# A hybrid encoder layer with 16 experts: expert weights loaded two chunks at a time

## What is computed

```
gates, idx = top_k(transpose(softmax(x @ w_router)), 64)      # each of 16 experts takes its 64 best tokens
xe  = x[idx]                                                  # 64 x 1024
hid = silu(xe @ w_gate[e]) * (xe @ w_up[e])                   # 1024 x 2048 each
ye  = (hid @ w_down[e]) * gates                               # 2048 x 1024
y[idx] += ye
```

## Time and profile before

| | us |
|---|---|
| median of 3 runs | 1295.26 |
| lowest, highest | 1293.75, 1296.32 |
| the profiled execution: its own time | 1294.17 |
| its span (first to last instruction) | 1292.4 |
| TensorE busy with matmuls | 1152.6 (89%) |
| packets of the SP queue's loads, share of 16 DMA engines | 81.0% |
| HBM read | 439.65 MB |

### The profile page before, as it was taken

One profiled execution on the slowest core, in us unless ns is written; L12 is line 12 of the kernel. 1 busy time (PEld: TensorE's weight loads), 2 busy tenths in 40 slices (PEclk: granted clock), 3 DMA queues, 4 the chain that ended last, 5 costly groups with the idle time before them and its releaser, 6 DMA issues.

```text
span 1292.4 us, 13555 instructions
## 1 busy us (share of the span) xinstructions
PE 1152.6 (89%) x5620; PEld 576.8 (45%) x5620; DVE 264.4 (20%) x465; ACT 191.4 (15%) x352; POOL 124.5 (10%) x61
## 2 busy tenths in 40 slices
PE   8999998989499999999889978997998899789874
PEld 6876777888453343333224322422432243234221
DVE  2012377637610020020002002000200020020005
ACT  4223434142100000000000001000000100010003
POOL 4412225321003000000000000000000000000003
PEclk9999999999699999999999999999999999999997
DMA  9432222163769999999999999999999999999992
GB/s 370 160 117 88 99 75 112 69 254 166 293 235 427 426 424 428 429 428 426 429 429 430 426 428 429 430 427 427 429 429 427 427 429 430 427 427 428 430 425 97
DMA packets 38030, 442.19 MB, mean 342 GB/s; under 512 B 6512, under 2 KB 6640, under 8 KB 10736
## 3 DMA queue, kind: packets, MB, share of 16 engines
q1 hardware_dynamic: 34512, 438.55, 81.0%
q10 hardware_dynamic: 3488, 3.22, 0.8%
HBM read 439.65 MB, written 2.10 MB: 342 GB/s over the span
## 4 chain that ended last, share of the span: by engine, by line
PE 72%; DMA 17%; DVE 6%; ACT 3%; issue 1%; POOL 1%; SPq 0%; POOLq 0%; ACTq 0%; DVEq 0%
PE bank L970 25%; DMA ring<-in_w_exp 16%; PE bank L992 16%; PE bank L929 5%; PE bank L1002 4%; PE bank L667 2%; PE bank L669 2%; PE bank L672 2%; PE bank L656 2%; ACT yt L618 1%; PE bank L979 1%; PE bank L804 1%; PE bank L805 1%; PE bank L806 1%; PE bank L648 1%
## 5 line engine op out<-in xcount | busy, mean ns | idle before, releaser
L970 PE MATMUL bank<-ring,yt 128*64 128x512 f32 x2048 | 452.7, 595 | 43.8 <-DMA ring<-in_w_exp 43.8
L970 PEld LDWEIGHTS bank<-ring,yt 128*64 128x64 f32 x2048 | 142.9, 137 | 336.0 <-issue 256.4
L992 PE MATMUL bank<-ring,yt 128*64 128x512 f32 x992 | 221.0, 595 | 29.4 <-ACT yt L618 22.6
L992 PEld LDWEIGHTS bank<-ring,yt 128*64 128x64 f32 x992 | 72.2, 137 | 158.4 <-issue 121.4
L1250 DVE TENSOR_TENSOR work<-bank,work 128x512 f32<-128x512 f32 x32 | 22.1, 692 | 445.6 <-PE bank L970 445.6
L615 ACT ACTIVATE work<-bank 128x512 f32<-128x512 f32 x32 | 19.1, 598 | 551.2 <-PE bank L970 551.2
L405 POOL TENSOR_SCALAR stat<-stat 128x1 f32<-128x1 f32 x3 | 1.7, 555 | 866.7 <-ACT work L633 866.7
L1256 DVE TENSOR_TENSOR xT<-bank,xT 128x512 f32<-128x512 f32 x64 | 44.3, 692 | 165.3 <-PE bank L1002 165.3
L929 PE MATMUL bank<-yt,res 128*128 128x128 f32 x512 | 63.3, 283 | 13.3 <-DVE yt L1236 13.3
L929 PEld LDWEIGHTS bank<-yt,res 128*128 128x128 f32 x512 | 60.3, 197 | 25.6 <-DVE xT L1256 17.7
L398 POOL TENSOR_TENSOR piece<-ring,piece 128x1024 fp32r<-128x1024 f32 x23 | 55.8, 2427 | 121.7 <-ACT piece L458 121.7
(11 more groups left out here) (164 smaller groups left out, 998.8 us busy)
## 6 DMA issues: line engine op xcount, KB each, us to landing
ring<-in_w_exp SPq DMA_DIRECT2D x182, 2048.0 KB, 30.3
ring<-in_dense SPq DMA_DIRECT2D x11, 2048.0 KB, 8.4
ring<-in_w_exp SPq DMA_DIRECT2D x16, 1024.0 KB, 32.9
ring<-in_x_turned SPq DMA_DIRECT2D x8, 256.0 KB, 5.6
res<-in_na_bias SPq DMA_DIRECT2D x1, 2048.0 KB, 24.3
res<-in_x SPq DMA_DIRECT2D x1, 2048.0 KB, 7.8
xT<-in_w_exp SPq DMA_DIRECT2D x1, 2048.0 KB, 9.2
out<-xT SPq DMA_DIRECT2D x4, 512.0 KB, 2.6
```

The costliest lines, as they stand in the source:

```text
L970: mm = nc.tensor.matmul(bank[2 * g + n % 2][64 * c:64 * c + 64, :], xeT[:, kk, 64 * e:64 * e + 64], exp_rhs(j, first, k, c), start=kk == 0 ...
L992: mm = nc.tensor.matmul(bank[5][64 * n:64 * n + 64, :], hidT[:, s, 64 * c:64 * c + 64], exp_rhs(j, first, s, n), start=(g, c, s) == (0, 0, ...
```

## The change

Two neighbouring chunks become one load. On the host they are laid side by side, so that a partition's 32 KB are contiguous; the ring is used as four double slots. `load_exp` takes even j only, issues one transfer of 4 MB and signals one semaphore per double slot. A refill waits until both chunks of the double slot are used. Chunks 22 and 23 of a pair come as 3 MB (22 and the first half of 23, `half_in`) and 1 MB. FIRST becomes 4, so that pairs start on even slots, and the loads ahead are regrouped: 0 and 1 after `mo_lo_split`, 2 and 3 after PJ_MO, 4 to 7 after PJ_MO + 8. TensorE waits at even chunks. The matmuls and their order are the same.

```diff
--- before.py
+++ after.py
@@ -24,7 +24,7 @@
 FMIN = float(np.finfo(np.float32).min)
 SLOT = 4096
 SLOTS = 8
-FIRST = 3
+FIRST = 4
 EXTRA = 8
 EXTRAS = 2
 CPE = 12
@@ -206,7 +206,7 @@
         mq_hi_split, mq_lo_split = sem("mq_hi_split"), sem("mq_lo_split")
         mo_hi_split, mo_lo_split, mem_hi = sem("mo_hi_split"), sem("mo_lo_split"), sem("mem_hi")
         att_hi, conv_gated, conv_hi, x1_hi = (sem(n) for n in ("att_hi", "conv_gated", "conv_hi", "x1_hi"))
-        exp_in = [sem(f"exp_in{s}") for s in range(SLOTS)]
+        exp_in = {s: sem(f"exp_in{s}") for s in range(0, SLOTS, 2)}
         extra_in = [sem(f"extra_in{n}") for n in range(EXTRAS)]
         half_in, y_started = sem("half_in"), sem("y_started")
         exp_used = sem("exp_used")
@@ -272,10 +272,14 @@
                 return scattered[k][2][:, 512 * c:512 * c + 512] if k < 3 else scattered[3 + c][2]
             return exp_chunk(j, first)[:, k, 512 * c:512 * c + 512]
 
-        chunks = experts.rearrange("c p (k n) -> c p k n", k=4)
-
         def exp_src(pair, j):
-            return chunks[bass.ds(CPP * pair + j, 1)].rearrange("c p k n -> (c p) k n")
+
+            two = experts[bass.ds(CPP // 2 * pair + j // 2, 1)]
+            return two.rearrange("c p (k n) -> (c p) k n", k=8)
+
+        def exp_room(j, first):
+            s = exp_slot(j, first)
+            return ring[:, s * SLOT:(s + 2) * SLOT].rearrange("p (k n) -> p k n", k=8)
 
         def edge_tokens(v):
 
@@ -299,13 +303,12 @@
                 sp.dma_start(pre_flat(c), dense[c]).then_inc(pre_in[PRE_SLOT[c]], 16)
 
             def load_exp(j, pair=0, first=True):
-                landed = extra_in[0] if first and j == EXTRA else exp_in[exp_slot(j, first)]
-                if j == CPP - 1:
-                    for h, semaphore in enumerate((half_in, landed)):
-                        sp.dma_start(exp_chunk(j, first)[:, 2 * h:2 * h + 2], exp_src(pair, j)[:, 2 * h:2 * h + 2])\
-                            .then_inc(semaphore, 16)
+                room, src, landed = exp_room(j, first), exp_src(pair, j), exp_in[exp_slot(j, first)]
+                if j == CPP - 2:
+                    for rows, semaphore in ((slice(0, 6), half_in), (slice(6, 8), landed)):
+                        sp.dma_start(room[:, rows], src[:, rows]).then_inc(semaphore, 16)
                     return
-                sp.dma_start(exp_chunk(j, first), exp_src(pair, j)).then_inc(landed, 16)
+                sp.dma_start(room, src).then_inc(landed, 16)
 
             def load_x(k):
                 sp.dma_start(x_raw[:, k, :], x_turned[:, k, :]).then_inc(x_in[k], 16)
@@ -352,29 +355,25 @@
             load_pre(CH_MQ)
             sp.wait_ge(projected, PJ_MQ)
             load_pre(CH_MO)
-            sp.wait_ge(mq_lo_split, MQ_GROUPS)
+            sp.wait_ge(mo_lo_split, MO_GROUPS)
             load_exp(0)
-            load_exp(1)
-            sp.wait_ge(mo_lo_split, MO_GROUPS)
+            sp.wait_ge(projected, PJ_MO)
             load_exp(2)
-            sp.wait_ge(projected, PJ_MO)
-            for m in range(3, 6):
-                load_exp(m)
             sp.wait_ge(projected, PJ_MO + 8)
+            load_exp(4)
             load_exp(6)
-            load_exp(7)
             sp.wait_ge(logits_done, 1)
-            load_exp(EXTRA)
+            sp.dma_start(exp_chunk(EXTRA, True), exp_src(0, EXTRA)[:, 0:4]).then_inc(extra_in[0], 16)
             for row, cols, room in scattered:
-                sp.dma_start(room, exp_src(0, EXTRA + 1)[:, row, cols]).then_inc(extra_in[1], 16)
-            for j in range(EXTRA + EXTRAS, CPP):
+                sp.dma_start(room, exp_src(0, EXTRA)[:, 4 + row, cols]).then_inc(extra_in[1], 16)
+            for j in range(EXTRA + EXTRAS, CPP, 2):
 
                 first_lot = j < EXTRA + EXTRAS + SLOTS
-                sp.wait_ge(exp_used, j - SLOTS + 1 - (EXTRAS if first_lot else 0))
+                sp.wait_ge(exp_used, j - SLOTS + 2 - (EXTRAS if first_lot else 0))
                 load_exp(j)
             with sp.Fori(1, PAIRS) as i:
-                for j in range(CPP):
-                    sp.wait_ge(exp_used, i * CPP + (j - SLOTS + 1))
+                for j in range(0, CPP, 2):
+                    sp.wait_ge(exp_used, i * CPP + (j - SLOTS + 2))
                     load_exp(j, i, first=False)
             for t in (0, 2, 1, 3):
                 if t < SCALED_TILES:
@@ -931,13 +930,20 @@
                 if k1 % 4 == 0:
                     mm.then_inc(mixed, 1)
 
+            def expert_all_in(i, j, first):
+                pe.wait_ge(exp_in[exp_slot(j, first)], i * (16 * CPP // SLOTS) + 16 * ((j - EXTRA - EXTRAS) // SLOTS + 2))
+
             def expert_in(i, j, first):
                 if first and EXTRA <= j < EXTRA + EXTRAS:
                     pe.wait_ge(extra_in[j - EXTRA], 16 * (1 if j == EXTRA else len(scattered)))
+                elif j == CPP - 2:
+                    pe.wait_ge(half_in, i * 16 + 16)
+                elif j % 2:
+                    pass
                 elif first and j < EXTRA:
                     pe.wait_ge(exp_in[exp_slot(j, first)], 16)
                 else:
-                    pe.wait_ge(exp_in[exp_slot(j, first)], i * (16 * CPP // SLOTS) + 16 * ((j - EXTRA - EXTRAS) // SLOTS + 2))
+                    expert_all_in(i, j, first)
 
             def pair(i, first):
                 pe.wait_ge(half_picked, i + 1)
@@ -981,13 +987,10 @@
                         pe.wait_ge(hidT_kept, i * 4 + (2 * e + g + 1))
                         for c in range(2):
                             j = CPE * e + 8 + 2 * g + c
-                            if j == CPP - 1:
-                                pe.wait_ge(half_in, i * 16 + 16)
-                            else:
-                                expert_in(i, j, first)
+                            expert_in(i, j, first)
                             for s in range(4):
                                 if j == CPP - 1 and s == 2:
-                                    expert_in(i, j, first)
+                                    expert_all_in(i, j - 1, first)
                                 for n in range(2):
                                     mm = nc.tensor.matmul(bank[5][64 * n:64 * n + 64, :], hidT[:, s, 64 * c:64 * c + 64],
                                                           exp_rhs(j, first, s, n),
@@ -1290,7 +1293,7 @@
         w = (gate, up)[n % 2][0].reshape(E, 2, 4, P, 2, 1024)
         out[:, n] = w[:, n % 4 // 2, :, :, n // 4].transpose(0, 2, 1, 3)
     out[:, 8:] = down[0].reshape(E, 4, 4, P, D).transpose(0, 1, 3, 2, 4)
-    return out.reshape(E * CPE, P, SLOT)
+    return out.reshape(E * CPE // 2, 2, P, SLOT).transpose(0, 2, 1, 3).reshape(E * CPE // 2, P, 2 * SLOT)
 
 
 def by_column(x):
```

## The result

Over 20 runs each the changed kernel takes 1296.79 us (1294.51 to 1299.21) and the kernel before 1295.25 (1293.75 to 1297.35): a ratio of 1.0014, 95% interval 1.0007 to 1.0020. The forecast was 1296.8. In the last experiment the unchanged source of the changed kernel was run again: 1297.62 against 1294.96, ratio 1.0016 (1.0007 to 1.0024). By the ratios the change costs 1.8 and 2.1 us (the medians differ by 1.5 and 2.7). Neither interval takes in 1, so the kernel is slower, by about as little as can be told from no change.

What follows compares the result with a forecast made beforehand. The expert part was taken as bound by a continuous DMA stream that TensorE follows. Start +4.9, cadence -6.9, tail +3.5 and ring 0 sum to +1.5 us, 1296.8 us, with a range of 1291 to 1304.

Steps and rivals of the forecast that it cites:

- The cadence: Steady stream of expert weights: 32 KB packets in place of 16 KB save 38 ns a chunk, -6.9 us over 181 chunks.
- The start: First refill: chunks 10 and 11 go together and wait for two used chunks, so one chunk more remains to move, +4.9 us.
- The tail: End of the last pair: TensorE starts chunks 20 and 21 only when both have landed, 15.6 us to the end, +3.5 us.
- The sum: Whole kernel: 4.9 - 6.9 + 3.5 + 0 = +1.5 us, giving 1296.8 us against the median.
- At nothing: Loads ahead of the stream: regrouped loads end at about 356, before chunk 0 is wanted at 363.07, so they cost nothing.
- the first boundary: Between the first two pairs: data end at 481.3, next double issued at 480.4 plus about 1 us; hole taken as 0.
- A granted clock under 1.00 in the stretch 485:1073: Sign that the forecast is wrong: TensorE's clock falls in the steady part, from longer waits.
- A first expert matmul later than 363: Sign that the forecast is wrong: TensorE's first expert matmul comes later than 363 us.
- The margin of 8 us: Ring at a pair's boundary: queue full until L + 38.9, next release at L + 30.8, L being chunk 23's landing.
- Rival 1: Stream's packets: longer rows bring little, cut at 16 KB or gap growing with size; +8.4 us, 1303.7; chance 0.27.
- Rival 2: Stream's packets: gaps go altogether or memory reads longer runs faster, -4.6 us, 1290.7; includes a fixed cost per transfer; chance 0.13.
- Rival 3: Ring at pair boundaries runs dry, each of seven losing a chunk's 4.9 us: 1331; chance 0.05.

Runs made afterwards that it cites:

- the experiment with 16 KB rows: Changed kernel with the same 4 MB transfers, waits and slots, but each partition gets two runs of 16 KB: 1303.88 us, ratio 1.0065 to the kernel before.
- the 8 KB rows: Kernel before with each 2 MB chunk laid out as two blocks, so a partition gets two runs of 8 KB: 1307.28 us, ratio 1.0090.
- the second profile: Profile from running the changed kernel's source again, nothing changed: 1297.62 us, ratio 1.0016 to the kernel before.
- three double slots: Changed kernel with each refill from the second pair on held back until two more chunks are used: 1337.87 us, ratio 1.0323 to the kernel before.
- the late start: Kernel before with chunk 10 waiting for two used chunks in place of one, all else in single chunks: 1300.23 us, ratio 1.0036.
- the second experiment: Changed kernel with the last four chunks of every pair as loads of 2, 2, 2, 1 and 1 MB: 1298.21 us, ratio 1.0017 to the kernel before.

## Why the prediction was right

**Right, with its sizes.** The cadence: 32 KB packets at 1216 ns (forecast 1216.4), 20,832 packets (some 20,800), a period of 116.6 us (116.6), and -6.9 us against 6.6 us by the experiment with 16 KB rows (5.8 by its stretch). The overlap of 3.5 ns a packet was a little large: 0.5% of 614.6 ns is 3.1, which leaves 9.7 ns, the value that the 8 KB rows gave in the steady part. The start: the first refill waits for chunk 1, and one chunk later costs 4.7 us when done alone (4.9). The tail: 15.5 us from the start of chunks 20 and 21 to the last matmul (15.6). The sum: +1.40 us in the stretch that the change touches, +1.5 in the medians, 1.8 and 2.1 by the two ratios, +1.5 forecast; and the traces give its parts, -2.1 us to the last data (-2.0) and +3.5 behind it. "At nothing" held for the loads ahead, which ended at about 359 (356 forecast): chunk 0 was not waited for, and the first expert matmul lies within 0.7 us of the other kernels' spread.

**Right in its sum, too simple in its reason.** "+4.9 us" was put down to the start alone. The two experiments on it read together: undone alone in the double ring it gives back 0.4 us in the stretch, done alone in the single ring it costs 4.1. The forecast had both numbers for the first boundary, 481.3 and 480.4 plus 1 us, and drew only the conclusion that no hole adds to the sum. The other half is that the boundary is a floor of its own. The same holds for the tail: it isn't the last double alone that is late, but TensorE behind from 18 and 19 on.

**Wrong in its signs.** Two of the signs named for "wrong" came, and the sum held. A granted clock under 1.00 in the stretch 485:1073 came (0.98), and TensorE's slack took it up: behind the slow group at 1236.64 the next wait is 0.84 us, where the second profile, without the slow group, has 2.54. A first expert matmul later than 363 came too (366.06 and 365.19), but that was no sign at all: the kernel before has 363.07 itself, and 364.89 with only its first refill held back. The margin of 8 us was too large by some 2 to 4, which cost nothing here.

**Rival 1** (longer rows bring little) falls: 8.4 to 9.7 ns a packet are measured, against the 3.5 ns worked out from the Trainium skill (DMA: Bandwidth & Descriptors, Why small descriptors are slow). The page's 3 cycles are the cost on one bus inside the engine; these runs see only the total and don't contradict that figure, but it is no estimate of what a packet costs in a stream. **Rival 2** falls with the 32 KB packet's 1216 ns. Its 2.0 us for each transfer are, in the Trainium skill (DMA: Bandwidth & Descriptors, Anatomy of one DMA), a fit for transfers that GpSimd issues, and those here are issued by SP; with 4 MB transfers of 16 KB rows the period stayed 117.5 us, so here no fixed cost of a transfer shows. **Rival 3** needed its margin gone; the experiment that took it away cost 40 us.

## What to carry to other kernels

In a stream of transfers that is never idle, a packet has a small price of its own, here 9 ns against 0.6 us for 16 KB, and longer contiguous rows earn 0.8% of the stream; but coarser transfers are paid where the queue is short: at its start, where the consumer pauses, and at the end. Count these in units of one transfer and compare them with the gain before making everything coarse, and go fine only there. When two limits coincide, undoing one shows nothing: look for the place where the queue runs dry in the experiment before calling the first cost false.

## What the runs showed of the hardware

TensorE's granted clock fell for short spells in the steady part of every kernel with doubles (down to 0.94 in stretches of 60 to 120 us), and not in the profiles of those with single chunks alone (the kernel before, the late start, the 8 KB rows: 1.00 in each such stretch). Busy time by stretch in the changed kernel:

```profile
core 0: us, PE busy (x) PEld busy (x) DVE busy (x) ACT busy (x) POOL busy (x), PEclk, DMA share, GB/s
1236.60:1245.40 8.80, 8.76 (x32) 3.15 (x32) 0.00 (x0) 0.00 (x0) 0.00 (x0) 0.81 0.98 421
1246.20:1253.30 7.10, 7.04 (x33) 2.23 (x33) 0.00 (x0) 0.60 (x1) 0.00 (x0) 1.00 1.00 430
```

```profile
1237.70:1241.10 3.40, 3.40 (x11) 1.20 (x8) 0.00 (x0) 0.00 (x0) 0.00 (x0) 0.50 1.05 453
```

In the second fence the stretch lies wholly in such a spell: a granted clock of 0.50, that is 1.2 GHz. TensorE had waited 2.72 us for a double before, after 1.89 us for the one before that (1226.83 in the same timeline). With single chunks its longest waits for a chunk were 1.3 us (1.4 in the 8 KB rows). A long wait doesn't decide it alone: in the same profile the groups at 1003.37 and 1120.01 come after waits of 2.73 and 2.72 us and take 7.09 us. What decides which groups are slow stays open. A spell costs 1.7 us in a group of 32 matmuls (8.78 against 7.09). It is hidden where a wait follows, and it isn't where TensorE sets the end or a release: in the second experiment's profile it lengthened the last chain by 1.5 us, and with three double slots it widened a hole. How much of the spread of the changed kernel's runs it makes was not tried.
